# Two-block mixer kernel on one core: projections between two steps of the inverse, a gate's tanh behind the values, the values' copy ahead of the keys' root, all in the first pair's iteration of block 2's recurrence

## The reference

```python
mod = silu(c) @ ada_w + ada_b
h = rmsnorm(x) * (1 + scale) + shift
p = h @ w_in                       # c_val, c_gate, c_og, ts, r_og, g_conv, g_rwkv
u = c_val * sigmoid(c_gate)        # then a causal depthwise convolution of 31 taps
r, k, v, w_low, a_low = token_shift(ts)
decay = exp(-exp(-softplus(-(w0 + tanh(w_low) @ w2)) - 0.5))
a = sigmoid(a0 + a_low @ a2)
kk = k * k_k / sqrt(sum(k*k_k squared over a head))
for each token t:
    sk = state @ kk_t
    state = state * decay_t - sk * (kk_t * a_t) + v_t * k_t
    out_t = state @ r_t
y_rwkv = (groupnorm(out) + bonus * v) * silu(r_og) @ w_o
```

## Time and profile before

| what | value |
|---|---|
| runs | 1120.84, 1121.67, 1121.72 us, median 1121.67 |
| the profiled execution: own time | 1121.51 us |
| its span, first to last instruction | 1119.4 us (2.1 us lie around it) |
| TensorE matmul busy | 1102.4 us, 98% |
| VectorE busy | 614.9 us, 55% |
| ScalarE busy | 227.3 us, 20% |
| GpSimd busy | 170.6 us, 15% |
| mean granted TensorE clock | 0.998 |
| DMA | 162.15 MB, 145 GB/s |
| iteration 0 of block 2's recurrence | about 641 to 685 us of the span |

### The profile page before, as it was taken

How to read it: one execution, slowest core, us unless ns; L and a number is a source line. 1 busy time by engine, 2 the same in 40 slices (tenths; PEclk the granted TensorE clock), 3 DMA queues, 4 the chain that set the end, 5 groups by cost and what they waited for, 6 DMA issues and landing times.

```text
span 1119.4 us, 21143 instructions
## 1 busy us (share of the span) xinstructions
PE 1102.4 (98%) x8798; PEld 931.6 (83%) x8798; DVE 614.9 (55%) x1433; ACT 227.3 (20%) x598; POOL 170.6 (15%) x214
## 2 busy tenths in 40 slices
PE   9999999999999999999999989999999999999997
PEld 8888888888888589999645878888888888887875
DVE  4252252523444367776547676567667667666424
ACT  4031130312200020110101431313223132323100
POOL 1100000000035214422470012020201202020000
PEclk9999999999999999999999999999999999999999
DMA  8666556460557347564564322323332322161241
GB/s 285 239 239 210 191 174 227 141 236 1 172 188 224 121 124 208 193 209 153 187 215 161 114 81 91 100 91 105 100 100 81 109 78 76 40 227 40 89 137 37
DMA packets 55312, 162.15 MB, mean 145 GB/s; under 512 B 8593, under 2 KB 14641, under 8 KB 55218
## 3 DMA queue, kind: packets, MB, share of 16 engines
q1 hardware_dynamic: 54210, 159.17, 42.8%
q10 hardware_dynamic: 1008, 1.63, 0.4%
HBM read 159.68 MB, written 1.11 MB: 144 GB/s over the span
## 4 chain that ended last, share of the span: by engine, by line
PE 92%; DVE 6%; DMA 1%; issue 1%; ACT 0%; SPq 0%; POOL 0%; DVEq 0%; POOLq 0%
PE bank L447 28%; PE bank L927 19%; PE bank L774 11%; PE bank L840 6%; DVE arena L2193 4%; PE bank L1084 3%; PE bank L587 2%; PE bank L1247 2%; PE bank L708 2%; PE bank L750 2%; PE bank L1071 1%; PE bank L902 1%; PE bank L962 1%; PE bank L523 1%; PE bank L908 1%; PE bank L478 1%
## 5 line engine op out<-in xcount | busy, mean ns | idle before, releaser
L927 PE MATMUL bank<-hT,slots 128*128 128x256 f32 x1120 | 254.8, 382 | 1.6 <-ACT arena L1502 1.3
L927 PEld LDWEIGHTS bank<-hT,slots 128*128 128x128 f32 x1120 | 209.7, 190 | 30.7 <-issue 2.4
L447 PE MATMUL bank<-hT,slots 128*128 128x256 f32 x1056 | 232.4, 380 | 1.2 <-DVE arena L1717 0.7
L447 PEld LDWEIGHTS bank<-hT,slots 128*128 128x128 f32 x1056 | 199.4, 190 | 29.6 <-issue 2.3
L2193 DVE SCALAR_TENSOR_TENSOR arena<-padA,par,arena 128x256 f32<-128x256 f32 x232 | 114.8, 559 | 0.0
L447 PE MATMUL bank<-arena,slots 128*128 128x256 f32 x432 | 94.6, 380 | 0.3 <-DVE arena L1855 0.2
L447 PEld LDWEIGHTS bank<-arena,slots 128*128 128x128 f32 x432 | 81.8, 190 | 12.4 <-issue 1.4
L2586 POOL TENSOR_TENSOR arena<-arena 128x256 f32<-128x256 f32 x40 | 33.7, 865 | 355.6 <-PE bank L902 302.3
L774 PE MATMUL bank<-arena,slots 128*128 128x128 f32 x640 | 79.6, 275 | 0.0
L774 PEld LDWEIGHTS bank<-arena,slots 128*128 128x128 f32 x640 | 75.8, 192 | 0.2
L1773 DVE SCALAR_TENSOR_TENSOR adaA<-arena,sc,adaA 128x1024 f32<-128x1024 f32 x24 | 30.3, 1282 | 55.2 <-DMA arena<-in_ada_w 55.2
(11 more groups left out here) (390 smaller groups left out, 1523.2 us busy)
## 6 DMA issues: line engine op xcount, KB each, us to landing
slots<-in_w_rwkv SPq DMA_DIRECT2D x72, 512.0 KB, 3.6
slots<-in_w_heads SPq DMA_DIRECT2D x68, 512.0 KB, 3.9
slots<-in_w_gu SPq DMA_DIRECT2D x44, 512.0 KB, 4.5
arena<-in_ada_w SPq DMA_DIRECT2D x24, 512.0 KB, 5.9
slots<-in_w_down SPq DMA_DIRECT2D x20, 512.0 KB, 4.0
slots<-in_w_br SPq DMA_DIRECT2D x32, 256.0 KB, 2.7
slots<-in_w_out SPq DMA_DIRECT2D x16, 512.0 KB, 3.8
slots<-in_w_y SPq DMA_DIRECT2D x16, 512.0 KB, 5.4
```

Source lines behind the costliest of these rows:

```text
L447: end = e.matmul(psum, w[:, k * P:(k + 1) * P], rhs[:, k, :], start=k == 0, stop=k == kt - 1)
L927: end = e.matmul(proj(w, q), slot[w][:, k * P:(k + 1) * P], hT[:, k, :], start=k == 0, stop=k == KT - 1)
```

## The change

Four edits, in iteration 0 only (j = 0; `chain` is false there and true in all others). TensorE runs five matmuls of the third fill between `grown(1)` with its products and `inverted(1)`, and four instead of nine afterwards. ScalarE computes `cth.1` right behind `hv.1`, before it waits for N.0, instead of behind `act_low_rank(1)`. And ScalarE runs a one-element square root (`sqrt_table`, L1265) and then the two copies of v.1 ahead of `act_kk(1)`, instead of `act_kk(1)` first.

```diff
             if levels:
                 grown(1)
                 products(e, chunks(bank[6][:, T:]), K, A).then_inc(*pe.step(f"M.{j}"))
+                if not chain:
+                    fill(5)
...
                 low_rank_mm(e, j + 1).then_inc(*pe.step(f"low.{j + 1}"))
-            fill(next(n))
+            fill(next(n) if chain else next(n) - 5)
...
             if j == 0:
                 act_value(e, 1)
+                act_gate(e, 1)
...
                 act_low_rank(e, j + 1)
-                act_gate(e, j + 1)
+                if j:
+                    act_gate(e, j + 1)
...
+            if j == 0:
+                sqrt_table(e, "kk")
+                act_pad(e, "v", V_, j + 1)
             if more:
                 act_kk(e, j + 1)
             if 1 < j < R_PAIRS:
                 act_group_norm(e, j - 2)
             if more:
-                act_pad(e, "v", V_, j + 1)
+                if j:
+                    act_pad(e, "v", V_, j + 1)
```

## The result

Twenty runs of the changed kernel have a median of **1123.67 us** (1120.57 to 1125.31), twenty of the kernel before 1121.74 (1120.76 to 1123.33). The ratio is **1.0014, 95% interval 1.0007 to 1.0020**: slower by 1.6 us by the ratio (the medians differ by 1.9), where 0.6 faster was forecast. The profiled execution took 1125.31 us, its span is 1123.1 (1119.4 before) and its mean granted clock 0.996 (0.998).

The account below looks back on a forecast made before the run. The prediction took TensorE, busy for 98% of the span, to bound the kernel. Gains of 0.53 us (first two edits) and 0.0 (values' copy) off the median of 1121.67 gave 1121.1 us, range 1120.1 to 1122.9.

Parts of the forecast that it names:

- The gate's tanh: ScalarE, iteration 0: table load hidden under the wait for GATE.1; N.0 and GpSimd 2.2 us later at no cost.
- The five matmuls: TensorE before `inverted(1)`: 2.26 us of fill removes both larger stalls; `inverted(1)` at 650.4, ready for `inverted(2)` at 655.5.
- What is late next: VectorE's ten taps hold G2: `inverted(2)` at 657.73 behind a 2.2 us stall, gain 0.53 us.
- The values' copy: ScalarE's root and v.1 copies: ROG.0's wait moves to `inverted(4)`, about 0.68 us there; worth 0.0 us.
- The sum: Whole kernel: gains of 0.53 and 0.0 us taken off the median of 1121.67, giving 1121.1 us.
- Rival 1: Behind the new stall before `inverted(2)` TensorE's clock falls; costs at most 2.6 us, 1122.8 to 1123.7; chance 0.16.
- VectorE beside GpSimd: Taps ahead of G1: GpSimd's later start makes the first two short, so G1 is done by 648.8, against 649.4.

Follow-up runs that it names:

- e1_no_split: The changed kernel without the split of the third fill, all nine matmuls behind `inverted(1)` again; 1119.13 us against 1122.20 for the kernel before, ratio 0.9971.
- e3_taps: The changed kernel with five of VectorE's ten taps moved ahead, between G1 and the copy of step 1; 1118.77 us against 1122.20 for the kernel before.
- e4_values_only: The kernel before with only the one-element root and the values' copies ahead of `act_kk(1)`; 1121.85 us against 1122.20, ratio 0.9999.
- e7_gate_only: The kernel before with the gate's early tanh alone; 1119.14 us against 1121.50, ratio 0.9979.
- e2_dummy: The changed kernel with four idle matmuls of constants just before `inverted(2)`; 1121.07 us against 1122.20 for the kernel before, ratio 0.9990.
- e5_split3: The changed kernel with three matmuls of the third fill ahead of `inverted(1)` and six behind; 1120.98 us against 1121.57 for the kernel before.
- e11_stall: The changed kernel without the split, with G2 made late by other VectorE work put ahead of it; 1124.08 us against 1121.50 for the kernel before, ratio 1.0027.
- e8: The changed kernel without the split, with three of seven taps ahead of G4 moved behind `operand_a`; 1118.34 us against 1121.57 for the kernel before.
- e9: The kernel before with two idle matmuls ahead of `inverted(1)` and two ahead of R_.1; 1121.28 us against 1121.57.

## Why the prediction was wrong

- **The gate's tanh** (load under cover, N.0 at 644.45, GpSimd 2.2 us later at no cost): right; 644.53, and no wait for GpSimd at `grown(1)`. Without the five matmuls the late GpSimd costs `inverted(1)` 0.15 us (e1_no_split).
- **The five matmuls** (`inverted(1)` at 650.4, TensorE ready at 655.5): right to 0.2; 650.60 and some 655.6.
- **What is late next** (VectorE's ten taps, `inverted(2)` at 657.73 behind a stall of 2.2 us): right; 657.89 and 2.29. e3_taps shows the cause.
- **The values' copy** (0.0 us): right, by e4_values_only and by e7_gate_only against e1_no_split (1119.14 and 1119.13). The wait it leaves before `inverted(4)` is 0.92 us, not about 0.68.
- **The sum** (1121.1): it is the time of the change where the clock holds: 1121.07 in e2_dummy, 1121.2 in the six of the changed kernel's 31 runs that have a mean clock of 0.999 or more. It isn't the change's time.
- **Rival 1, where it failed.** The sum prices the new stall as idle time alone and has no term for the clock behind it; that cost stood only in rival 1. There mechanism, place and point of decision were written down: a stall of 2.2 us, as long as the one after which the clock fell at the kernel's end. The chance of 0.16 was the error. "Busy work stands close on both sides" was an argument without a row. No stall of this trace over 1.3 us stood between busy work, so nothing spoke for holding, and one row spoke for falling. Long falls alone come in 14 of 31 runs. The price, "2.6 at most", was too low as well: 3.27 us in one profiled execution and 3.26 in the other. I took it from the kernel's first 24 matmul records, which lose 2.6 us; but the windows of the kernel before give a granted clock of 1.00 for its first 10 us, so no row shows a low clock there, nor how long one lasts. Here it lasted 6.8 us in both. And the range doesn't take in "most of rival 1", as the prediction says: that rival's times begin at 1122.8 and end at 1123.7, and the range ends at 1122.9. So 1123.67, a time that the rival had named, lay outside it.
- **What I had in hand and didn't use.** The part on VectorE beside GpSimd has G1 ready 0.6 us sooner (648.8 against 649.4) because of the tanh alone; it came 1.1 sooner. Even the 0.6 is half of the first stall. Followed to its end, that says that this stall needs little fill, and that a fill of 2.26 us can only hold `inverted(1)` and with it the ten taps. Without the fill the gain is 2.5 us.

Why a given execution falls and another of the same stall holds stays open; the runs show shares, not a rule.

## What to carry to other kernels

Two small stalls of TensorE apart can be cheaper than one as long as both: here merging them brought `inverted(2)` 0.4 us forward and cost 3.3 in clock where the clock fell. When a change leaves TensorE waiting amid busy work for about as long as here (a fall was seen behind 1.42 us, the shortest stall tried), count the work behind it at half clock in a good share of executions, and shorten the stall, or fill it even with idle matmuls. Before filling a stall, look whether another edit of the same change already makes its releaser early.

## What the runs showed of the hardware

- In four profiled executions the granted clock fell from 2.4 to 1.2 GHz behind stalls of 1.42, 2.29 (twice) and 2.82 us between busy work; in a fifth, with 1.86 us, it held. The fall began 2.4 to 4.5 us after TensorE went idle, 0.2 to 1.7 us after it was busy again. The clock stayed at half for 3.4 us (e5_split3, e11_stall) or 6.8 (the changed kernel, both times) although TensorE was busy throughout. The Trainium skill's page "TensorE: Matmul & The Clock Gate", section "Why this matters for your kernels", warns only of idle gaps between bursts that are longer than any of these stalls; the traces differ, and the measurement decides.
- Long falls (mean clock 0.996 or less) by the longest stall that the profile has in this iteration: 0 of 51 runs at under 1 us (e1, e2, e3, e7, e8, e9), 7 of 90 at two stalls of 1.2 and 1.3 us (the kernel before, e4), 0 of 11 at 1.42, 2 of 11 at 1.86, 14 of 31 at 2.29, 5 of 11 at 2.82. Elsewhere every one of these kernels has a stall or two of 0.9 to 1.2 us.
- A tap on VectorE takes 0.40 us while GpSimd rests, and about 0.9 beside GpSimd's instructions: the last three of the six taken together take 2.71 us in e3_taps (its timeline of VectorE from 646 us),

```profile
645.17 2.71 DVE L2201 SCALAR_TENSOR_TENSOR arena<-padA,par,arena 128x256 f32<-128x256 f32 x3
```

so the later start of GpSimd, which is off the critical path, made VectorE's G1 a microsecond earlier.
